# A two-layer hybrid trunk on one core: experts' gather ahead of a branch with its test turned round, attention parameters in the gates' stage, one split behind the merged quarters

## What is computed

```python
for l in range(2):
    h = rmsnorm(x, norm1_g[l]); proj = h @ w_in[l]
    br = [pool_mixer(...), diff_attention(...), conv_module(...), spatial_gating(...)]
    br = einsum('bsic,icd->bsid', br, w_branch[l])
    gates = sigmoid(h @ w_gate[l] + b_gate[l])
    x = x + sum_i(gates_i * br_i) @ w_out[l]
    h2 = rmsnorm(x, norm2_g[l])
    x = x + (swiglu(h2) if l == 0 else moe_ffn(h2))     # moe: top 2 of 8 experts per token
# in diff_attention:
lam = exp(sum(lq1 * lk1)) - exp(sum(lq2 * lk2)) + lam_init
a = p[:, 0] - lam * p[:, 1]
o = rmsnorm(o, subln_g) * (1.0 - lam_init)
```

## Time and profile before

| What | Value |
|---|---|
| median of 3 runs | 1555.28 us (1554.86 to 1558.85) |
| the profiled execution | 1556.29 us, of which its span is 1554.6 us |
| PE busy | 1509.8 us, 97% of the span |
| weight loads on PE | 1277.0 us, 82% |
| DVE busy | 1279.2 us, 82% |
| ACT busy | 1097.4 us, 71% |
| granted PE clock, mean | 0.993 of full speed |
| read from HBM | 457.89 MB, 295 GB/s over the span |

### The profile page before, as it was taken

How to read it: one execution, slowest core, us unless ns; L and a number is a source line. 1 busy time by engine, 2 the same in 40 slices (tenths; PEclk the granted TensorE clock), 3 DMA queues, 4 the chain that set the end, 5 groups by cost and what they waited for, 6 DMA issues and landing times.

```text
span 1554.6 us, 22647 instructions
## 1 busy us (share of the span) xinstructions
PE 1509.8 (97%) x8593; PEld 1277.0 (82%) x8593; DVE 1279.2 (82%) x1423; ACT 1097.4 (71%) x1314; POOL 18.0 (1%) x34
## 2 busy tenths in 40 slices
PE   8999999999999998799999999999999999999998
PEld 7999969999899996688777788777888777888675
DVE  5887765555577966698899998999988999988997
ACT  5675453333558562487899977889877889877896
POOL 4000000000000000000000000000000000000000
PEclk9999999999999999899999999999999999999999
DMA  9544345555453451699999999999999999999993
GB/s 273 192 160 167 135 160 201 186 186 190 148 198 144 165 187 41 247 421 415 355 413 418 421 421 359 358 399 417 421 408 359 367 392 418 421 391 346 382 406 163
DMA packets 64873, 460.50 MB, mean 296 GB/s; under 512 B 7434, under 2 KB 7670, under 8 KB 9462
## 3 DMA queue, kind: packets, MB, share of 16 engines
q1 hardware_dynamic: 63878, 457.22, 74.7%
q0 software_dynamic: 832, 1.74, 0.8%
q10 hardware_dynamic: 48, 0.02, 0.0%
HBM read 457.89 MB, written 1.05 MB: 295 GB/s over the span
## 4 chain that ended last, share of the span: by engine, by line
PE 76%; DVE 15%; ACT 5%; issue 2%; DMA 1%; SPq 0%; DVEq 0%; ACTq 0%
PE bank L1083 9%; PE bank L1087 9%; PE bank L1084 9%; PE bank L778 9%; DVE w_lo L615 9%; PE bank L779 9%; PE bank L780 9%; PE bank L1036 6%; PE bank L1039 6%; DVE w_lo L551 2%; PE bank L1115 2%; PE bank L1048 2%; PE bank L1123 2%; ACT w_hi L543 1%; DMA ring<-in_w_in 1%
## 5 line engine op out<-in xcount | busy, mean ns | idle before, releaser
L615 DVE TENSOR_TENSOR w_lo<-arena,w_hi 128x1024 fp32r<-128x1024 f32 x527 | 619.7, 1226 | 42.4 <-ACT w_hi L609 36.9
L609 ACT ACTIVATE w_hi<-arena 128x1024 fp32r<-128x1024 f32 x527 | 535.0, 1056 | 81.7 <-PE bank L1087 67.5
L551 DVE TENSOR_TENSOR w_lo<-ring,w_hi 128x2048 fp32r<-128x2048 f32 x94 | 215.1, 2291 | 146.3 <-ACT w_hi L543 145.0
L778 PE MATMUL bank<-h_hi,w_hi 128*128 128x256 f32 x992 | 283.2, 285 | 4.1 <-DVE w_lo L551 2.4
L779 PE MATMUL bank<-h_lo,w_hi 128*128 128x256 f32 x992 | 280.6, 283 | 0.0
L780 PE MATMUL bank<-h_hi,w_lo 128*128 128x256 f32 x992 | 280.6, 283 | 0.0
L543 ACT ACTIVATE w_hi<-ring 128x2048 fp32r<-128x2048 f32 x94 | 179.9, 1915 | 109.1 <-PE bank L780 79.7
L778 PEld LDWEIGHTS bank<-h_hi,w_hi 128*128 128x128 f32 x992 | 190.2, 192 | 6.3 <-issue 2.9
L779 PEld LDWEIGHTS bank<-h_lo,w_hi 128*128 128x128 f32 x992 | 190.3, 192 | 0.5
L780 PEld LDWEIGHTS bank<-h_hi,w_lo 128*128 128x128 f32 x992 | 190.2, 192 | 0.0
L1083 PE MATMUL bank<-w_hi,h_hi 128*128 128x512 f32 x448 | 176.9, 395 | 0.0
(11 more groups left out here) (303 smaller groups left out, 2215.9 us busy)
## 6 DMA issues: line engine op xcount, KB each, us to landing
arena<-in_moe_w SPq DMA_DIRECT2D x270, 1024.0 KB, 8.3
ring<-in_moe_w SPq DMA_DIRECT2D x66, 1024.0 KB, 8.3
ring<-in_ffn_w SPq DMA_DIRECT2D x33, 1024.0 KB, 4.8
ring<-in_w_gate SPq DMA_DIRECT2D x32, 1024.0 KB, 4.8
ring<-in_w_in SPq DMA_DIRECT2D x15, 1024.0 KB, 6.5
ring<-in_w_branch SPq DMA_DIRECT2D x8, 1024.0 KB, 4.7
ring<-in_w_out SPq DMA_DIRECT2D x8, 1024.0 KB, 4.8
x_tok<-in_x SPq DMA_DIRECT2D x2, 512.0 KB, 4.3
```

The source lines that it names most:

```text
L551: nc.vector.tensor_tensor(w_lo[:, m % LO, :], raw, w_hi[:, m % HI, :].bitcast(F32), ALU.subtract)\
L609: nc.scalar.activation(half_hi[:, r % AHEAD, :], raw_of(n)[:, HALF * (m % 2):HALF * (m % 2) + HALF], ACT.Copy)\
L615: eng.tensor_tensor(half_lo[:, r % AHEAD, :], raw_of(m // 2)[:, HALF * (m % 2):HALF * (m % 2) + HALF], half_hi[:, r % AHEAD, :].bitcast(F3 ...
L778: pe.matmul(out_, a[0], b[0], start=start, stop=False)
```

## The change

- The two gathers of the first expert move from the start of `gathered_experts` on PE to a place ahead of the branch.
- The branch's test is turned round on PE, ACT and DVE: `gathered_experts` is now the body that follows the test directly, and `all_tokens` stands behind it, as the other case.
- DVE's parameters `subg` and `lams` move to gate 3, ACT's exponential to gate 4, DVE's `neglam` to gate 5. All of it in layer 0.
- DVE's low part of `out` unit 1 moves behind the four quarters of the last branch, in both layers, and each `m_lo` stands ahead of the low part of its unit.
- On ACT the call that switches to the square root before layer 1 is written at the end of the dense feed-forward instead of in `norm`. ACT's instructions and their order there stay the same: the split that the shorter `hi_until` leaves out had been made by the call before it.

```diff
             def gathered_experts():
-                for c in range(2):
-                    gather(0, c, 5 + 2 * c)
...
             most_tokens = pe.value_load(most_i[0:1, 0:1])
-            with pe.If(most_tokens > CAP):
+            for c in range(2):
+                gather(0, c, 5 + 2 * c)
+            with pe.If(most_tokens < CAP + 1):
+                gathered_experts()
+            with pe.Else():
                 all_tokens()
-            with pe.Else():
-                gathered_experts()
...
-                step(fn(rms0[:, 0:1], eps[:, :], ACT.Sqrt))
+                if n != 2:
+                    step(fn(rms0[:, 0:1], eps[:, :], ACT.Sqrt))
...
+                if g == 4 and l == 0:
+                    act_e.wait_ge(lam_summed, 1)
+                    fn(lame[:, :, :], lams[:, :, :], ACT.Exp).then_inc(lam_exped, 1)
...
                         if w == "w2" and s == nsteps:
-                            hi_until(plan.split[plan.index[ukey]] + HI - 1)
+                            step(fn(rms0[:, 0:1], eps[:, :], ACT.Sqrt))
+                            hi_until(plan.split[plan.index[ukey]] + 1)
...
                     elif w == "cg":
-                        if l == 0:
-                            act_e.wait_ge(lam_summed, 1)
-                            fn(lame[:, :, :], lams[:, :, :], ACT.Exp).then_inc(lam_exped, 1)
                         copy_out(key, sig[:, :, :], ACT.Sigmoid)
...
                     dve.wait_ge(attn_loaded, 16 * ATTN)
-                    for j in range(L):
-                        step(ts(subg[:, j, :], subg[:, j, :], 1.0 - lam_init[j], None, ALU.mult))
-                    lam_sums()
...
-                if l == 0:
-                    dve.wait_ge(lam_exped, 1)
-                    for j in range(L):
-                        last = stt(out=neglam[:, j:j + 1], in0=lame[:, j, 1:2], scalar=-lam_init[j], in1=lame[:, j, 0:1],
-                                   op0=ALU.add, op1=ALU.subtract)
-                    step(last)
...
+                    if g == 3 and l == 0:
+                        for j in range(L):
+                            step(ts(subg[:, j, :], subg[:, j, :], 1.0 - lam_init[j], None, ALU.mult))
+                        lam_sums()
+                    if g == 5 and l == 0:
+                        dve.wait_ge(lam_exped, 1)
+                        for j in range(L):
+                            last = stt(out=neglam[:, j:j + 1], in0=lame[:, j, 1:2], scalar=-lam_init[j], in1=lame[:, j, 0:1],
+                                       op0=ALU.add, op1=ALU.subtract)
+                        step(last)
...
-                    lo_until(min(at(("branch", l, i)) + LO_AHEAD, at(("branch", l, BR_ORDER[-1])) + int(n == 3)))
+                    lo_until(min(at(("branch", l, i)) + LO_AHEAD, at(("branch", l, BR_ORDER[-1]))))
...
                 for u in range(1, 4):
+                    m_lo(l, u)
                     lo_until(at(("out", l, u)))
-                    m_lo(l, u)
```

More of the change, by code:

```diff
@@ L1581, in _ @@
             most_tokens = act_e.value_load(most_i[0:1, 0:1])
-            with act_e.If(most_tokens > CAP):
+            with act_e.If(most_tokens < CAP + 1):
+                gathered_experts()
+            with act_e.Else():
                 all_tokens()
-            with act_e.Else():
-                gathered_experts()
         @block.vector
@@ L2171, in _ @@
             most_tokens = dve.value_load(most_i[0:1, 0:1])
-            with dve.If(most_tokens > CAP):
+            with dve.If(most_tokens < CAP + 1):
+                gathered_experts()
+            with dve.Else():
                 all_tokens()
-            with dve.Else():
-                gathered_experts()
 _INS = ['x', 'norm1_g', 'w_in', 'w_gate', 'b_gate', 'w_branch', 'w_out', 'pool_w', 'pool_scale', 'attn_qn_g', 'attn_kn_g',
```

## The result

The changed kernel takes 1543.63 us, the median of four runs (1541.70 to 1546.21), against 1555.07 for the kernel before beside it. The ratio is 0.9924, with a 95% interval of 0.9901 to 0.9947: faster by 11.4 to 11.8 us, with some 3.6 to either side. The forecast was 1542.0 us, with a range of 1540 to 1548. The profiled execution took 1544.31, its span is 1542.6 us, so 12.0 less than before.

A forecast was written before the change was run, and what follows sets the result against it. PE, busy 97% of its time, was taken as the bound. 1.55 + 4.4 + 2.8 + 5.0 − 0.4 = 13.35 us off the profiled 1556.29 gives 1542.9, and 1542.0 as that run stood 1.0 above the median; range 1540 to 1548.

The forecast's parts named there:

- Parameters, +1.55: Layer 0's attention parameters moved to the gates: PE's 2.38 us gap shrinks by 1.8, `combine` costs 0.25; bounds 1.0 and 1.9.
- The slowing by POOL that the next instructions might inherit: At the parameters' old place on DVE: if POOL slows DVE, the next instruction may inherit up to 0.8 us.
- The cover on ACT: At gate 4: 2.8 us of exponential and table loads on ACT, covered by 0.2 to 0.4 before DVE's low part.
- Low part, 4.4: Ahead of `out` unit 0: PE's gap shrinks from 2.66 to 0.45 us, 2.2 in each layer; 3.5 if banks come later.
- The rival with 4.4 lost: At `out` unit 1: it waits for its moved low part as long as the gap was; 1546.4 us, chance 0.04.
- Clock, 2.8: Over `out` unit 0: the shorter gap keeps PE's clock up, 1.4 us in each layer; bounds 0 and 2.8.
- The experts' start, 5.0: Gathers ahead of the turned branch: the experts start 5.0 us earlier, with transfers as the limit; bounds 2.0 and 5.5.
- The rival that PE runs at 1.2 GHz: At the experts' start, while PE is needed: 5.0 becomes 2.0, giving 1545.0 us; chance 0.14.
- The rival of a cold instruction stream behind the gathers: At the experts' start: turning the test does nothing for PE, the pauses come after the gathers; 1547.0 us, chance 0.08.
- The end's jump, −0.4: Behind DVE's last sum: a 3.75 us jump with 2.5 to 2.9 us of cover costs 0.4; bounds 0 and −6.1.
- a sign of being wrong: At the program's end: the prediction is wrong if the span runs on 5 us or more behind the last sum.
- the bound with both pauses: At the end's jump: if DVE pays both of PE's pauses, 9.0 us, the cost is 6.1.

The follow-up runs named there:

- the low part alone: The kernel before with only DVE's low part of `out` unit 1 moved behind the quarters; ratio 0.9952, 7.5 us less.
- the sums behind the join: The changed kernel with DVE's last four sums taken out of the body and put behind the join, under a second test; ratio 0.9909 to the kernel before.
- all tests as before: The changed kernel with the tests on PE, ACT and DVE put back as they were, the other edits kept; ratio 0.9914 to the kernel before.
- the experts' part alone: The kernel before with only the gathers ahead of the branch and the test turned on PE, ACT and DVE; ratio 0.9964, 5.6 us less.
- the gathers alone: The kernel before with only the gathers moved ahead of the branch, the test as it was; ratio 0.9973, 4.2 us less.
- the turned test alone: The kernel before with only the test turned on PE, ACT and DVE, the gathers still behind it; ratio 0.9981, 3.0 us less.

## Why the prediction was right, and where it was off

The mechanism of each part held but that of the end's jump, and the time lies in the range. Some of the sizes were off.

1. **Parameters, +1.55.** The DVE side was exact: from the low part before to the one that PE waits for it is 9.40 us before (34.18 to 43.58) and 7.59 after (32.97 to 40.56), 1.8 us. The slowing by POOL that the next instructions might inherit is 0.36 of the 2.17: the two products with `qkg` take 1.60 beside POOL now, 1.29 without it before. PE's gap shrinks by only 1.5 in the mean of the traces, since it was 1.8 in the mean of five and not 2.38. The 0.25 at `combine` was 0.22. The cover on ACT was 0.3 as worked out. This term measures 1.2 over all traces, and 1.6 in this pair, whose gap before was long.
2. **Low part, 4.4.** 2.2 in each layer, as worked out: gaps of 0.46. The moved split at 193.64 to 195.92 ends 0.15 us before `out` unit 1 at 196.07, and nothing waits. The rival with 4.4 lost is out.
3. **Clock, 2.8.** The gap ahead of `out` unit 0 lowers the clock, as supposed, and each stage got back 1.7, where 1.4 was worked out. But the step "another 2.8" took for granted that a clock kept here stays kept. In the changed kernel the router's matmuls in layer 1 ran at the lower level, and the 1.7 of layer 1 were gone by the counts. The table's third line says it: 37.41 against 37.43, and it is 35.7 in the kernel with the low part alone. Over the router the granted clock was this, after and with the low part alone:

```profile
614.80:620.20 5.40, 4.86 (x24) 4.68 (x24) 2.35 (x7) 2.10 (x4) 0.00 (x0) 0.62 0.01 3
```

```profile
617.80:621.40 3.60, 3.10 (x24) 2.89 (x24) 2.25 (x7) 2.00 (x4) 0.00 (x0) 1.00 0.02 5
```

The same 24 matmuls are spread over 5.4 us or 3.6. In the kernel before they had 0.97. Of the seven kernels with the gap of 0.46, three (the changed one, the sums behind the join, all tests as before) take 37.4 to 37.6 us from `out` 0 of layer 1 to the counts, and four 35.4 to 35.8. The term measures 1.7 in the changed kernel's trace, 3.4 with the low part alone. The Trainium skill (TensorE: Matmul & The Clock Gate, "What's actually happening") has activity release the throttle; the traces agree in that the clock stayed up at all fourteen places where the gap had shrunk to 0.46, and they show that it can be low again at the next thin stage, behind a gap of 1.88.

4. **The experts' start, 5.0.** Measured 5.25 from the counts to the last sum, 6.0 with this part alone. The transfers are the limit, as argued: PE's first half came 7.6 us sooner (10.47 for 18.03 behind the counts), and 2.3 of it were gone by the last sum. The size came in part by luck. The second transfer landed 6.9 us after its issue and not 8.4, so the low part of the third half starts 13.04 us behind the counts in place of 19.90, 6.9 sooner and not 5.5. Most of what was lost again went within the first two steps: PE stands 0.57 us for a low part at 643.73, and ACT waits for a transfer before each pair of its high parts there. And 0.7 went at the end, where from 1528 to 1532 the granted clock is 0.72; with the experts' part alone it is 1.00 in its place, and the start is worth 6.0. The rival that PE runs at 1.2 GHz was half true. It did so over the gathers (a clock of 0.67 from 628.3 to 633.5), and it cost nothing that the traces show. The rival of a cold instruction stream behind the gathers is out: no "issue" row is left.

5. **The end's jump, −0.4.** This step failed: it costs 2.2, and the span ran on for 5.4 us behind the last sum, which the prediction had named as a sign of being wrong. I priced DVE's jump behind the last sum, with one pause of 3.75. What makes the end late is PE's, which starts at 1534.4, before its last matmuls are through. Its 3.94 us end at 1538.3, behind the last sum, and the span runs on to 1542.6. So the step "a jump can begin as soon as the sum is issued" named the wrong engine, and the bound with both pauses was right for PE: 1534.4 to 1542.6 is 8.2 us, nearly the 9.0 that I had put on DVE. That the second pause is the same as the 5.25 at the start is borne out by q8: each of the two has one transfer of PE's instructions in it.

The sum in this pair of traces: 1.6 + 4.4 + 1.7 + 5.25 − 2.2 = 10.75, against 13.35 forecast. The end took 1.8 more than forecast and the clock gave 1.1 less; the experts gave 0.25 more. The other 1.2 of the 12.0 stand ahead of the first edited instruction (the low part at 34.18 starts at 32.97 now), in code that is the same: scatter, which helped the forecast by luck. The prediction's best bounds add to 14.6 and not 14.8, which changes nothing.

## What to carry to other kernels

A gap of PE costs more than its length if the clock falls behind it: here some 2.65 us idle brought 1.4 to 3.1 more at nine of twelve places. But a clock kept at one thin stage can be low at the next, so count it as a gain only where the trace shows it kept to the end of the thin stages.

Turning a branch's test moves the far jump, it does not remove it. An engine that jumps at the end, and the two pauses that belong to the jump, should be through before the last store lands. PE, which is the bound here, starts its jump 8.2 us before the span's end, and that is too late. Before more is built on such an edit, look whether work that both cases share can stand ahead of the branch; here that alone gave as much in the total, within what can be measured.

## What the runs showed of the hardware

- A jump past some 6,100 rows of PE's program takes 3.5 to 3.9 us on its sequencer (5.9 to 6.2 where it starts under queued gathers). With the pause that follows it is 9.7 us at the start, and the span's end comes 1.4 to 2.3 later, while a test that isn't taken takes 0.09 us. Two transfers on the queue of PE's instructions go with it. On DVE the far jump at the start shows as 5.7 to 6.0 us of "issue", with a row of 0.07 for the test. The Trainium skill (Advanced Engine Details and Errata, "Control Flow Timing") gives about 108 ns for a compare-and-branch: the 92 ns of the one not taken are near it, the 3.5 us and more of the far one are not.
- Two scalings of 64 columns on DVE (`subg`) took 1.23 us beside POOL's affine select, and 0.42 at their new place with POOL idle. It is POOL and not the place: in the kernel with the gathers alone they stand at the old place, POOL's select is over 2 us before them, and they take 0.41.
- The same code scatters by several us: PE reaches `out` 0 of layer 0 between 193.0 and 194.9 us in four kernels that are the same up to there, and needs 398.7 to 403.7 us from there to layer 1's. The level of the clock in thin stages makes part of this: from there to layer 1 the kernel with the turned test alone has 0.93 from 218 to 243 us and 0.91 from 393 to 418, the kernel with the gathers alone 1.00 in both.
